# Three MLPs in split fp32: the first layer's high weight part meets both activation parts in one 512-column matmul

## The reference

```python
ff = jnp.square(jax.nn.relu(h @ w_ff_in[l])) @ w_ff_out[l]                  # first block
x = x + g2 * (jnp.square(jax.nn.relu(h @ mlp_w1[i])) @ mlp_w2[i])           # second block, i = 0, 1
mod = cond @ ada_w[i] + ada_b[i]                                            # modulation, 1024 x 6144 a layer
```

## Time and profile before

| | |
|---|---|
| median of 3 runs | 1093.14 us (1093.11 to 1094.69) |
| the profiled execution | 1095.8 us, of which the span from the first to the last instruction is 1094.0 us |
| mean granted TensorE clock | 0.989 of full speed |
| busy | PE 96%, PEld 84%, DVE 64%, ACT 45%, POOL 10% of the span |
| matmuls of 256 columns in unit_w | 3 x 992, of them 2304 in the MLPs |

### The profile page before, as it was taken

How to read it: one execution, slowest core, us unless ns; L and a number is a source line. 1 busy time by engine, 2 the same in 40 slices (tenths; PEclk the granted TensorE clock), 3 DMA queues, 4 the chain that set the end, 5 groups by cost and what they waited for, 6 DMA issues and landing times.

```text
span 1094.0 us, 16799 instructions
## 1 busy us (share of the span) xinstructions
PE 1049.3 (96%) x6872; PEld 924.3 (84%) x6872; DVE 701.1 (64%) x823; ACT 491.8 (45%) x553; POOL 111.4 (10%) x76
## 2 busy tenths in 40 slices
PE   6999998999999999998899999999998799999998
PEld 6997776799999998985789999998886579999996
DVE  4858556687666778654578666687574648454463
ACT  5355546444444446331454343445444744444441
POOL 0031002001001002024001000100000401100000
PEclk9999999899999999999999999999999899999999
DMA  8884335828878783786229787873553224556540
GB/s 281 314 291 159 128 116 160 287 79 315 288 254 288 272 281 106 220 257 197 86 74 341 264 288 259 288 266 134 193 192 123 109 78 155 192 185 198 185 161 39
DMA packets 118716, 221.58 MB, mean 203 GB/s; under 512 B 6338, under 2 KB 20740, under 8 KB 118660
## 3 DMA queue, kind: packets, MB, share of 16 engines
q1 hardware_dynamic: 116944, 214.97, 57.9%
q0 software_dynamic: 1520, 5.77, 1.6%
q10 hardware_dynamic: 196, 0.05, 0.0%
HBM read 215.07 MB, written 1.05 MB: 198 GB/s over the span
## 4 chain that ended last, share of the span: by engine, by line
PE 82%; DVE 7%; ACT 4%; issue 3%; DMA 2%; SPq 1%; ACTq 0%; DVEq 0%
PE ps L407 77%; ACT hi L345 2%; PE ps L868 2%; DVE lo L356 1%; PE ps L444 1%; DVE ada_acc L891 1%; DMA ada_raw<-in_ada_w 1%; PE ps L722 1%; PE ps L648 1%; DVE stat L1915 1%; DMA raw<-in_w_in 0%; DVE hTl L494 0%; PE ps L1192 0%; ACT aS L1626 0%; DVE aS L1910 0%
## 5 line engine op out<-in xcount | busy, mean ns | idle before, releaser
L356 DVE TENSOR_TENSOR lo<-raw,hi 128x2048 fp32r<-128x2048 f32 x153 | 356.1, 2334 | 274.8 <-ACT hi L345 274.0
L345 ACT ACTIVATE hi<-raw 128x2048 fp32r<-128x2048 f32 x153 | 292.2, 1913 | 331.1 <-PE ps L407 314.0
L407 PE MATMUL ps<-hTh,hi 128*128 128x256 f32 x992 | 282.7, 285 | 2.0 <-DVE hTl L494 1.9
L407 PE MATMUL ps<-hTh,lo 128*128 128x256 f32 x992 | 280.7, 283 | 0.0
L407 PE MATMUL ps<-hTl,hi 128*128 128x256 f32 x992 | 280.7, 283 | 0.0
L407 PEld LDWEIGHTS ps<-hTh,hi 128*128 128x128 f32 x992 | 190.3, 192 | 3.8 <-DVE hTl L494 2.5
L407 PEld LDWEIGHTS ps<-hTl,hi 128*128 128x128 f32 x992 | 190.3, 192 | 0.3
L407 PEld LDWEIGHTS ps<-hTh,lo 128*128 128x128 f32 x992 | 190.3, 192 | 0.0
L407 PE MATMUL ps<-hi,hidh 128*128 128x512 f32 x416 | 163.0, 392 | 0.4 <-DVEq L643 0.4
L407 PE MATMUL ps<-hi,hidl 128*128 128x512 f32 x416 | 162.1, 390 | 0.0
L407 PE MATMUL ps<-lo,hidh 128*128 128x512 f32 x416 | 162.1, 390 | 0.0
(11 more groups left out here) (216 smaller groups left out, 873.6 us busy)
## 6 DMA issues: line engine op xcount, KB each, us to landing
raw<-in_mlp_w SPq DMA_DIRECT2D x64, 1024.0 KB, 5.3
ada_raw<-in_ada_w SPq DMA_DIRECT2D x44, 1024.0 KB, 7.3
raw<-in_w_in SPq DMA_DIRECT2D x21, 1024.0 KB, 7.3
raw<-in_w_ff_in SPq DMA_DIRECT2D x16, 1024.0 KB, 5.4
raw<-in_w_ff_out SPq DMA_DIRECT2D x16, 1024.0 KB, 6.7
raw<-in_attn_w_qkv SPq DMA_DIRECT2D x12, 1024.0 KB, 5.4
raw<-in_conv_w_in SPq DMA_DIRECT2D x8, 1024.0 KB, 6.4
taps<-u_pad SPq DMA_DIRECT2D x64, 71.0 KB, 4.1
```

What stands on the lines that cost most here:

```text
L345: nc.scalar.activation(hi[:, slot], raw[:, slot], ACT.Copy).then_inc(hi_made, 1)
L356: nc.vector.tensor_tensor(lo[:, slot], raw[:, slot], hi[:, slot].bitcast(F32), ALU.subtract).then_inc(lo_made, 1)
L407: return nc.tensor.matmul(o, lhs, rhs, start=start, stop=False, skip_group_check=True)
```

## The change

The activations' two parts now lie side by side in one tile hT, high then low for each k. In the MLPs' first layers one matmul of 512 columns takes a high weight block over both parts (high x high into columns 0 to 255 of a bank, high x low into 256 to 511), and one of 256 columns takes the low block over the high part. Each of the four column tiles now has a bank of its own, 4 to 7, so ada_sum (bank 6) and `first` now share banks, and new waits order them: ada_sum waits for `summed`, and first waits at its third column tile (ct == 2) for the ada_keep of the ada_sum before it. Between the layers ACT first copies the low halves to relu (low_of), DVE adds the high halves (sum_of), and ACT then takes relu in place. At the head, banks 6 and 7 also hold the transposed activations, so the third column tile of unit u0 waits for all eight hT parts.

```diff
+        hT = place("hT", [P, KT, 2, SEQ], F32R)
+        hTh, hTl = hT[:, :, 0], hT[:, :, 1]
...
+        def unit_wide(pe, u, j, k0, ready=None):
+
+            slot = slot_of(u, j)
+            pe.wait_ge(lo_made, u + 1)
...
+            for ct in range(4):
+                if ct == 2 and ready is not None:
+                    pe.wait_ge(*ready)
+                c = slice(ct * P, (ct + 1) * P)
+                for k in range(4):
+                    mm(pe, ps[:, 4 + ct], wh[:, k, c],
+                       hT[:, k0 + k].rearrange("p h n -> p (h n)"), k0 == 0 and k == 0)
+                    last = mm(pe, ps[:, 4 + ct, 0:SEQ], wl[:, k, c], hTh[:, k0 + k])
+            last.then_inc(used, 1)
...
             pe.wait_ge(hT_lo, 8 * (2, 5, 8)[m] + 4)
-            unit_w(pe, u0, None, hTh, hTl, 0, 4, True)
-            pe.wait_ge(hT_lo, 8 * (2, 5, 8)[m] + 8)
-            unit_w(pe, u0 + 1, None, hTh, hTl, 4, 4, False)
+            unit_wide(pe, u0, None, 0, (hT_lo, 8 * (2, 5, 8)[m] + 8))
+            unit_wide(pe, u0 + 1, None, 4)
...
+            pe.wait_ge(summed, 8 * m + 1)
             ada_sum(pe, ADA_HEAD[m][0])
 
-            def first(c, u, j, chunk):
-                pe.wait_ge(relu_done, chunk)
-                unit_w(pe, u, j, hTh, hTl, 0, 4, True)
-                unit_w(pe, u + 1, j + 1, hTh, hTl, 4, 4, False)
+            def first(u, j, chunk, kept):
+                pe.wait_ge(summed, chunk)
+                unit_wide(pe, u, j, 0, kept)
+                unit_wide(pe, u + 1, j + 1, 4)
+
+            def kept_of(number):
+                return ada_kept, number + 2
...
                 if m < 2:
-                    ada_sum(pe, ada_loop(m, i)[0][0])
-                first(2, n + 4, s + 4, 2 * i + (8 * m + 2))
+                    pe.wait_ge(summed, 2 * i + (8 * m + 2))
+                    ada_sum(pe, a)
+                first(n + 4, s + 4, 2 * i + (8 * m + 2), kept_of(a) if m < 2 else None)
...
-            def relu_of(chunk):
-                nc.scalar.activation(relu[:], ps[:, 4:6].rearrange("p b n -> p (b n)"),
-                                     ACT.Relu).then_inc(relu_done, 1)
+            def low_of(chunk):
+                if not isinstance(chunk, int) or chunk:
+                    act.wait_ge(sq_done, chunk)
+                nc.scalar.activation(relu[:].rearrange("p (c n) -> p c n", c=4), ps[:, 4:8, SEQ:2 * SEQ],
+                                     ACT.Copy).then_inc(low_kept, 1)
 
             def hi_of(par_, chunk):
+                act.wait_ge(summed, chunk + 1)
+                nc.scalar.activation(relu[:], relu[:], ACT.Relu).then_inc(relu_done, 1)
                 act.wait_ge(sq_done, chunk + 1)
...
+            def sum_of(chunk):
+                dve.wait_ge(low_kept, chunk + 1)
+                r4 = relu[:].rearrange("p (c n) -> p c n", c=4)
+                nc.vector.tensor_tensor(r4, r4, ps[:, 4:8, 0:SEQ], ALU.add).then_inc(summed, 1)
+
             dve_step(dve, u0)
+            sum_of(8 * m)
             dve_step(dve, u0 + 1)
...
+                    if j % 4 == 1:
+                        sum_of(chunk + j // 4)
                     dve_step(dve, u + j, j=s + j)
                     if j % 4 == 1:
                         lo_of(1 - j // 4, chunk + j // 4)
```

More of the change, by code:

```diff
@@ L129, in build_kernel @@
         X = place("X", [P, TT, D])
-        hTh = place("hTh", [P, KT, SEQ], F32R)
-        hTl = place("hTl", [P, KT, SEQ], F32R)
+        hT = place("hT", [P, KT, 2, SEQ], F32R)
+        hTh, hTl = hT[:, :, 0], hT[:, :, 1]
         hid_area = area("hid", 16384)
@@ L270, in build_kernel @@
         relu_done = sem("relu_done")
+        low_kept = sem("low_kept")
+        summed = sem("summed")
         sq_done = sem("sq_done")
@@ L403, in unit_w @@
                         last = mm(pe, o, wl[:, k, c], act_h[:, k0 + k])
+            last.then_inc(used, 1)
+        def unit_wide(pe, u, j, k0, ready=None):
+            slot = slot_of(u, j)
+            pe.wait_ge(lo_made, u + 1)
+            wh = hi[:, slot].rearrange("p (k n) -> p k n", k=4)
+            wl = lo[:, slot].rearrange("p (k n) -> p k n", k=4)
+            for ct in range(4):
[6 more added lines that the diff above has]
+                    last = mm(pe, ps[:, 4 + ct, 0:SEQ], wl[:, k, c], hTh[:, k0 + k])
             last.then_inc(used, 1)
@@ L762, in mlp_pe, with tail_sum @@
                 n, s = 8 * i + (u0 + 2), u0 + 2
-                first(1, n, s, 2 * i + (8 * m + 1))
+                if m < 2:
+                    a, b = (ada_loop(m, i)[q][0] for q in range(2))
+                first(n, s, 2 * i + (8 * m + 1), kept_of(a + -1) if m < 2 else kept_of(ADA_HEAD[m][0]))
                 second(0, n + 2, s + 2, 2 * i + (8 * m + 1))
                 if m < 2:
-                    ada_sum(pe, ada_loop(m, i)[0][0])
-                first(2, n + 4, s + 4, 2 * i + (8 * m + 2))
+                    pe.wait_ge(summed, 2 * i + (8 * m + 2))
+                    ada_sum(pe, a)
+                first(n + 4, s + 4, 2 * i + (8 * m + 2), kept_of(a) if m < 2 else None)
                 second(1, n + 6, s + 6, 2 * i + (8 * m + 2))
                 if m < 2:
-                    ada_sum(pe, ada_loop(m, i)[1][0])
+                    pe.wait_ge(summed, 2 * i + (8 * m + 3))
+                    ada_sum(pe, b)
             n = u0 + 26
-            first(7, n, n, 8 * m + 7)
-            second(0, n + 2, n + 2, 8 * m + 7,
-                   (lambda: ada_sum(pe, ADA_TAIL[m][0]), (lambda: gate_row(pe, m - 1, 1)) if m else None))
+            first(n, n, 8 * m + 7, kept_of(ada_loop(m, 2)[1][0]) if m < 2 else None)
+            def tail_sum():
+                pe.wait_ge(summed, 8 * m + 8)
+                ada_sum(pe, ADA_TAIL[m][0])
+            second(0, n + 2, n + 2, 8 * m + 7, (tail_sum, (lambda: gate_row(pe, m - 1, 1)) if m else None))
             def last_sum():
@@ L795, in mlp_act @@
             act.wait_ge(used, u0 + 2)
-            relu_of(8 * m)
+            low_of(8 * m)
             act_step(act, u0 + 1)
@@ L803, in body @@
                         act.wait_ge(used, u + (j + 1))
-                        relu_of(chunk + j // 4)
+                        low_of(chunk + j // 4)
                     act_step(act, u + j, j=s + j)
@@ L939, in mlp_dve @@
                     ada_unit(dve, ADA_LAST[m][0], 1, skip(m))
+                if j == 1:
+                    sum_of(8 * m + 7)
                 dve_step(dve, u0 + 26 + j)
```

## The result

| | before | after |
|---|---|---|
| median | 1093.25 us (4 runs) | 1142.22 us (4 runs, 1141.8 to 1144.3) |
| ratio | | 1.044, 95% interval 1.0427 to 1.0453 |
| span of the profiled execution | 1094.0 us | 1140.1 us |
| mean granted TensorE clock | 0.989 | 0.971 |

The change makes the kernel 49 us slower. The forecast was 1133 us.

The account below looks back on a forecast made before the run. TensorE, busy 96% of the span, was taken as the bound. Terms -8.4 + 30.8 + 11.0 + 1.3 + 5.1 = +39.8 took the median from 1093.14 to 1133 us (3.6% slower), range 1112 to 1151.

Parts of the forecast that it names:

- the change doesn't do what it says: Rival: the wide-narrow mixture costs 0.360 a triple as before; +8.4, 1141 us; chance 0.06.
- Part 2, the loop: Loops of MLPs 0 and 1: later DVE results make TensorE wait 2.57 us at 12 places, +30.8 us.
- the turns of square and lo(u+5): Loop: POOL's square waits for DVE's lo(u+5), running from 5.08 to about 6.93; chance of no turn-taking 0.12.
- the two waits: Loops of MLPs 0 and 1: TensorE idles about 1.6 before ada_sum and 0.6 in mid-unit for ada_keep.
- I price none there: Loop: no clock loss priced, since waits of 1.6 and 0.6 lie below the 1.70 that did no harm.
- the idle of 1.70: An earlier TensorE idle after which the clock stayed 1.00; after one of 2.62 it was 0.57 over 4 us.
- The rival to which I gave 0.15: Clock also falls in the loop: two waits near an idle of 2.6, 1.7 each, +20, 1153 us; chance 0.15.
- Part 1, the pair: MLPs' first layers: one wide replaces two narrow matmuls, saving 0.0126 us a pair, 0.20 a unit, -8.4 us over 42 units.
- Part 3, the heads: MLP heads: sum_of behind lo(u0+4) on DVE delays first(1) by 3.35, 3.81 and 3.83, +11.0 us.
- The clock's share: Three heads: idle of about 4 us is followed by a clock of 0.57, losing 1.7 each, +5.1 us.
- Part 4: Tail and clock: DVE loses 1.3 us behind MLP 0, MLP 1's covered by gate rows; heads' clock loss +5.1 us.
- Faster: Rival: the vector chain keeps up and TensorE waits at none of 15 places; 9.6 gained, 1083.5 us; chance 0.04.

Follow-up runs that it names:

- ada_before_lo_of: The changed kernel with the second ada half ahead of lo_of in DVE's queue in the loops; 1124.3 us, ratio 1.0268.
- keep_early: The changed kernel with ada_keep ahead of lo(u+7) instead of behind it in DVE's queue, in the loops; 1137.1 us, ratio 1.0391.
- loops_reordered: The changed kernel with second ada half ahead of lo_of and ada_keep ahead of lo(u+7) in the loops, heads as changed; 1108.3 us, ratio 1.0109.
- lo_waits_square: The changed kernel with lo(u+5) on DVE held until POOL's square of the chunk is done, in the loops; 1144.5 us, ratio 1.047.
- warm_loop: The changed kernel with 6 calls of useless matmuls (1.4 us) in the wait ahead of every ada_sum in the loops; 1140.7 us, ratio 1.0426.
- before_reordered: The kernel before the change with second ada half ahead of lo_of, ada_keep ahead of lo(u+7) and lo(u0+5); 1094.1 us, ratio 1.0003.
- all_reordered: The changed kernel with chunk 0 narrow, second ada half ahead of lo_of, ada_keep ahead of lo(u+7) and lo(u0+5); 1089.0 us, ratio 0.9949.
- warm_heads_short: The changed kernel with 14 calls of useless matmuls (3.2 us) in the wait of each MLP's head; 1138.9 us, ratio 1.0415.
- narrow_heads: The changed kernel with chunk 0 of each MLP done as before the change, the other 7 chunks wide; 1138.5 us, ratio 1.0405.
- changed_again: The changed kernel measured once more, unedited, beside the kernel before; 1142.6 us, ratio 1.0442.

## Why the prediction was right or wrong

The direction, the range and the mechanism held; the size came out 9 us short, 49 us where 40 were forecast. The time lies near the 1141 of the rival *the change doesn't do what it says*, but by chance: a wide-narrow pair takes 0.3465 or 0.3533, not the 0.360 of that rival. By its parts:

- **Part 2, the loop.** The chain was right to 0.1 us at each step in the first half pass of MLP 1, the turns of square and lo(u+5) among them. Predicted half pass 25.5, measured 25.6 to 25.7 where the clock held (4 of 12). ada_before_lo_of and keep_early take out the two waits one at a time, and loops_reordered, without both, has none of the loss left in the loops; lo_waits_square shows the turns. The net forecast for 12 places was 30.8 - 4.8 = 26.0 us, the trace shows 33.6. The mis-sized term is the one that the forecast set to nothing: "I price none there", of the clock. It fell at 8 of 12 places, which adds 0.7 each, 5.6 us; the rest, 1.9, is mostly the pair price and the restart behind the keep, for which the prediction had no row: 0.15 forecast, 1.51 - 0.70 - 0.54 = 0.27 measured. My comparison with the idle of 1.70 looked at the wait alone. Behind the 1.5 to 1.6 of wait there is a microsecond of one-column matmuls (1.57 + 1.05 = 2.62 at 627.09, as long as the idle of the earlier trace rows behind which the clock was low). That these matmuls are what makes the difference is not shown: no run varied them, and the 1.70 is a single place. The rival to which I gave 0.15 was right that the clock falls, and wrong about the second wait, which isn't needed (keep_early) and isn't enough (warm_loop). Its price, 1.7 a place, was too high: on the lower clock TensorE reaches the third column tile after the keep, so that wait goes away in exchange. warm_loop shows this too: no lower clock, all places at 25.4 to 25.7, ada_keep waited for at all 12. What makes one place keep the clock and the next, with the same work, lose it is open.
- **Part 1, the pair.** 0.0126 saved a pair was forecast, from two uniform streams. Both that and half of it occur, and the changed kernel is mostly at the half: MLP 2's loop gains 1.1 us instead of 2.4. before_reordered shows that this saving, and not the order, is what all_reordered gains. Three narrow take 3 x 0.1199 = 0.3597, so a pair saves 13.2 or 6.4 ns against them.
- **Part 3, the heads.** first(1) starts 3.3, 4.4 and 4.5 us later than before, counted from the transposes (3.35, 3.81, 3.83 forecast); in MLPs 1 and 2 the ada_sum itself already runs on the lower clock, 1.72 and 1.86 us long instead of about 1.0. With first(1) the heads lose 16.8 us, against 16.1 less 1.2 of the gain that first(1) has. The clock's share, 5.1 in the forecast, is 7.0 by the trace of warm_heads_short, and 3 by its median. DVE as the one that sets it (sum_of behind lo(u0+4)) is what the waits name, 11.1 us for L953. That the loss could be had back by a narrow chunk 0 alone was wrong, as narrow_heads shows: the keep stands behind it.
- **Part 4.** MLP 0's end lost 1.3, as forecast, MLP 1's 0.6 where I had nothing.
- **Outside the MLPs** nothing was forecast, and the changed kernel is 5 us shorter there than the one profiled execution before. 2.6 of it is that execution, the rest is unexplained. It hides part of the shortfall: in the MLPs alone the loss is 51.2, 11.4 above the forecast's 39.8. Of these are 7.6 the loops, 1.3 MLP 2, 1.9 the heads, 0.6 the end of MLP 1.

"Faster" would have needed all waits below 9.6 us. all_reordered reaches that point, by undoing part of the change and by an order on DVE that the change didn't bring; there the gain is 5 us.

## What to carry to other kernels

- A cheaper matmul form that takes all PSUM banks turns resources that were apart into ones that are handed over. List every reader of the banks it takes over (here the modulation sums in bank 6), and find for each where its instruction stands in its engine's queue: here the two that mattered stood behind work that nobody was waiting for, and moving two lines was worth 34 us, with the heads repaired 53.
- When you ask whether a wait costs clock, look at what stands behind it as well: an idle of 1.70 left the clock at 1.00 in the earlier trace rows, yet here 1.5 to 1.6 with a microsecond of one-column matmuls behind it was followed by the lower clock at 6 to 8 of 12 places. Then price each wait again once the clock has slowed what follows it. Removing a wait may show another behind it; look for it before the run.

## What the runs showed of the hardware that was not expected

- A stream of alternating 512- and 256-column matmuls, each with new weights, ran here at full clock at one of two prices, 0.3465 or 0.3533 us a pair, constant until something interrupts the stream. On the lower clock a pair took 0.64, 0.29 more and not quite twice as long, here in keep_early (301.93 - 301.29):

```profile
301.29 0.63 PE L425 MATMUL ps<-hT,hi 128*128 128x512 f32 x1
...
301.93 0.63 PE L425 MATMUL ps<-hT,hi 128*128 128x512 f32 x1
```

- Behind a wait of 1.57 and an ada_sum of 1.05 the clock stayed at 1.00 in one half pass; behind 1.49 and 1.05 it was at 0.50 in the next, with the same work. 8 of 12 such places lost it, 7 of 12 in changed_again and 6 of 12 in keep_early, where no second wait follows; with the wait filled by matmuls of 128 columns, none.
